# GpSimd in place of VectorE for the softmax weights of one attention

## The reference, cut to what matters

```python
def swa_sink_attention(q, k, v, sinks):          # heads 0 to 7
    ...
    p = jax.nn.softmax(jnp.concatenate([s, sink], axis=-1), axis=-1)[..., :-1]
    o = jnp.einsum('bnkgqs,bnskd->bnqkgd', p.astype(vb.dtype), vb)

def dsa_attention(q, k, v, iq, ik, iw):          # heads 8 to 15
    ...
    _, idx = lax.top_k(score, n_top)
    ...
    p = jax.nn.softmax(s, axis=-1)
    o = jnp.einsum('bhqk,bqkd->bqhd', p.astype(vg.dtype), vg)

def mixer_ab(h, cos, sin, w_in, q_norm, w_uq, w_uiq, sinks, w_out):
    ...
    return jnp.concatenate([ya, yb], axis=-1) @ w_out
```

## Time and profile before

| | |
|---|---|
| time, median of 3 runs | 1816.06 us (1815.35 to 1817.51) |
| profiled execution | 1816.24 us, of which the span of the engines 1814.3 us |
| PE busy | 1743.7 us, 96% of the span |
| DVE busy | 749.0 us, 41% |
| ACT busy | 526.5 us, 29% |
| POOL busy | 26.6 us, 1%, 36 instructions |
| mean granted TensorE clock | 0.992 |

### The profile page before, as it was taken

How to read it: one execution, slowest core, us unless ns; L and a number is a source line. 1 busy time by engine, 2 the same in 40 slices (tenths; PEclk the granted TensorE clock), 3 DMA queues, 4 the chain that set the end, 5 groups by cost and what they waited for, 6 DMA issues and landing times.

```text
span 1814.3 us, 24405 instructions
## 1 busy us (share of the span) xinstructions
PE 1743.7 (96%) x9906; PEld 1092.5 (60%) x9906; DVE 749.0 (41%) x1287; ACT 526.5 (29%) x698; POOL 26.6 (1%) x36
## 2 busy tenths in 40 slices
PE   8999999999999999999999999999899999999997
PEld 7688754444434434343434344375699888679986
DVE  4454342212212112121212121379865469676555
ACT  5344421111111111111111010248444453744442
POOL 0002000000000000000000000000000000000001
PEclk9999999999999999999999999998999999999999
DMA  9958899999999999999999999974355556435550
GB/s 350 348 212 336 316 404 426 428 427 428 428 428 428 428 428 428 429 429 428 428 429 428 429 429 429 418 282 177 116 186 185 192 194 228 153 116 185 185 208 24
DMA packets 96608, 587.43 MB, mean 324 GB/s; under 512 B 7150, under 2 KB 7364, under 8 KB 70948
## 3 DMA queue, kind: packets, MB, share of 16 engines
q1 hardware_dynamic: 95072, 582.27, 79.3%
q10 hardware_dynamic: 1476, 4.30, 0.7%
HBM read 585.51 MB, written 1.05 MB: 323 GB/s over the span
## 4 chain that ended last, share of the span: by engine, by line
PE 72%; DMA 20%; DVE 5%; ACT 2%; issue 1%; SPq 0%; DVEq 0%; ACTq 0%
PE bank L1274 31%; DMA ring<-in_w_gate_up 19%; PE bank L1587 15%; PE bank L1606 9%; PE bank L1533 4%; PE bank L1861 3%; PE bank L1353 1%; PE bank L1617 1%; PE bank L1265 1%; PE bank L1579 1%; DVE w_lo L565 1%; ACT arena L965 1%; DMA ring<-in_ada_w 1%; PE bank L1599 1%; PE bank L1988 0%
## 5 line engine op out<-in xcount | busy, mean ns | idle before, releaser
L1587 PE MATMUL bank<-ring,arena 128*64 128x512 f32 x2048 | 462.4, 597 | 28.4 <-DMA ring<-in_w_gate_up 27.8
L1587 PEld LDWEIGHTS bank<-ring,arena 128*64 128x64 f32 x2048 | 137.7, 136 | 319.3 <-issue 255.9
L1606 PE MATMUL bank<-ring,arena 128*64 128x512 f32 x1024 | 226.8, 595 | 3.3
L1274 PE MATMUL bank<-w_hi,arena_r 128*128 128x512 f32 x672 | 217.1, 391 | 1.9 <-DVE arena_r L2705 1.9
L565 DVE TENSOR_TENSOR w_lo<-ring,w_hi 128x4096 fp32r<-128x4096 f32 (+2 forms) x44 | 192.5, 4375 | 44.1 <-ACT w_hi L554 41.8
L2400 DVE TENSOR_SCALAR arena<-bank 128x512 f32<-128x512 f32 x32 | 22.1, 691 | 367.2 <-PE bank L1587 367.2
L963 ACT ACTIVATE arena<-arena,sb_tab 128x512 f32<-128x512 f32 x32 | 23.1, 722 | 508.7 <-DVE arena L2400 508.7
L554 ACT ACTIVATE w_hi<-ring 128x4096 fp32r<-128x4096 f32 (+2 forms) x43 | 152.3, 3583 | 31.6 <-DMA ring<-in_c_w_out 18.3
L1606 PEld LDWEIGHTS bank<-ring,arena 128*64 128x64 f32 x1024 | 71.9, 137 | 137.6 <-issue 132.1
L1274 PE MATMUL bank<-XT_r,w_hi 128*128 128x256 f32 x512 | 145.8, 285 | 4.4 <-DVE arena_r L2689 4.4
L1274 PE MATMUL bank<-arena_r,w_hi 128*128 128x256 f32 x512 | 144.9, 283 | 0.0
(11 more groups left out here) (415 smaller groups left out, 2104.6 us busy)
## 6 DMA issues: line engine op xcount, KB each, us to landing
ring<-in_w_gate_up SPq DMA_DIRECT2D x128, 2048.0 KB, 32.0
ring<-in_w_down SPq DMA_DIRECT2D x64, 2048.0 KB, 35.3
ring<-in_mlp_w SPq DMA_DIRECT2D x32, 2048.0 KB, 8.3
ring<-in_ada_w SPq DMA_DIRECT2D x21, 2048.0 KB, 13.1
ring<-in_c_w_in SPq DMA_DIRECT2D x6, 2048.0 KB, 7.7
ring<-in_w_in SPq DMA_DIRECT2D x4, 2048.0 KB, 8.8
ring<-in_w_v SPq DMA_DIRECT2D x2, 2048.0 KB, 9.6
ring<-in_w_out SPq DMA_DIRECT2D x2, 2048.0 KB, 11.9
```

What stands on the lines that cost most here:

```text
L1274: mm = pe.matmul(out, st[a], mv[b], start=start and a + b == 0, stop=stop and a == 1, skip_group_check=True)
L1587: mm = pe.matmul(B[m][CAP * h:CAP * h + CAP, :], xe[:, 2 * j + kl, :], w[:, kl, m * D + h * HW:m * D + (h + 1) * HW], start=False, stop=(j ...
L1606: mm = pe.matmul(B[2][CAP * h:CAP * h + CAP, :], hT[:, c, CAP * j:CAP * j + CAP], w[:, c, h * HW:(h + 1) * HW], start=(j == 0 and c == 0), ...
```

## The change

In attention `ab` alone, VectorE's weights step ends with the reciprocals, which raise a new semaphore `ab_recip`. GpSimd waits for it and multiplies in place, in four operations for each unit, one for each head and half of the queries' tokens: two of 128 x 128 and two of 128 x 256, each with one tensor input and one reciprocal per partition. The second and the fourth raise `p`. From unit 2 on VectorE waits before its reciprocals until GpSimd has done unit u-2, as their places are used in turn. GpSimd's loop over the 8 units stands between its operation L777 and its wait for `late_read` 2, so its four small operations on the last modulation come behind unit 7. The other attention, `cc`, stays as it is.

```diff
             last = mod[:, 3, :]
             pool.wait_ge(sem("late_read"), 1)
             pool.tensor_tensor(mod[:, 2, 16:24], mod[:, 2, 16:24], ada_bT[:, 64:72], ALU.add).then_inc(sem("late_mod"), 1)
+            for u in range(ATTNS["ab"][0]):
+                pool.wait_ge(sem("ab_recip"), u + 1)
+                c, sc = 4 * (u % 2), SCORES["ab"][u % 3]
+                for t, (a, b) in enumerate(((0, P), (P, 3 * P))):
+                    for h in range(2):
+                        i = 8 + c + 2 * t + h
+                        ins = pool.tensor_scalar(sc[:, h, a:b], sc[:, h, a:b], att[:, 0, i:i + 1], None, ALU.mult)
+                    ins.then_inc(sem("p"), 1)
             pool.wait_ge(sem("late_read"), 2)
...
                     dve.wait_ge(*upto(st, "e", exps_of(st, u + 1)))
                     if u < ATTNS[st][1]:
                         link(dve.tensor_tensor(att[:, 2, c:c + 4], att[:, 2, c:c + 4], att[:, 4, c:c + 4], ALU.add))
+                    if st == "ab":
+                        if u >= 2:
+                            dve.wait_ge(*upto(st, "p", 2 * u - 2))
+                        dve.reciprocal(att[:, 0, 8 + c:12 + c], att[:, 2, c:c + 4]).then_inc(sem("ab_recip"), 1)
+                        return
                     link(dve.reciprocal(att[:, 0, 8 + c:12 + c], att[:, 2, c:c + 4]))
```

## The result

The changed kernel takes 1822.65 us, median of 6 runs (1821.31 to 1823.72), against 1815.3 us for the kernel before (6 runs, 1812.4 to 1817.51): ratio 1.0042, interval 1.003 to 1.0054, some 7 us slower. Forecast were 1816.7 us and no difference that can be measured; the measured time lies above the range of 1815.2 to 1819.7 us. Timed twice more beside the kernel before, it was slower by a ratio of 1.0073 (1.0056 to 1.009) and 1.0056 (1.0039 to 1.0073), in the medians by 12.4 and 9.9 us.

What follows compares the result with a forecast made beforehand. No single engine was taken to bound the stage, but a chain of handovers up to VectorE's first split; 2d - 0.28 = +0.66 us on the median 1816.06 gave 1816.7 us, range 1815.2 to 1819.7.

Steps and rivals of the forecast that it cites:

- The price of GpSimd's four operations: Attention ab, each unit: 1.45 us priced from GpSimd's casts, bounds 0.8 and 2.5 us.
- Slow GpSimd without the collision: Rival: GpSimd takes 2.0 to 2.5 us per unit, +1.8 to +2.8 us, about 1819.0 us; chance 0.05.
- d: Added latency from reciprocal to finished weights, for each unit whose transposes wait: 1.53 us against 1.06, +0.47 us.
- 2d - 0.28: Whole attention: d at units 0 and 4, less unit 2's 0.28 us wait for VectorE; +0.66 us.
- with 0.4 us to spare: Unit 3: GpSimd done near 1262.4 us, before TensorE wants the weights at 1262.67 + 0.19; delay hidden.
- Unit 7: Its transposes move by 1.1 us, hidden in 2.86 us between TensorE's projection end and VectorE's last bank.
- Nothing: Unit 1: transposes stand behind a TensorE projection and are copied behind ScalarE's second 3.6 us rounding; no delay.
- The relief: Two multiplications off VectorE per unit, 8.2 us over 8 units, worth only 0.28 us at unit 2's transposes.
- rival gain: VectorE's relief reaches the end as ScalarE binds less; at most 3.1 us less, 1813.0 us; chance 0.05.
- The collision: Rival: from 2.5 us per unit, GpSimd's last operation of unit 7 stands behind VectorE's first split; +6.4 us, 1822.6; chance 0.13.
- The clock: Rival: longer waits at units 4 to 7 bring 7 us of TensorE at half speed, 3.3 us, 1820; chance 0.05.
- ScalarE stood idle between 1247 and 1266 us: Sign that the forecast is wrong: VectorE was then the bound, and the relief counts.

Runs made afterwards that it cites:

- e3_forms: Changed kernel with GpSimd's operations in four forms by unit: the change's, times a constant, plain copy, two-input multiplication by the broadcast reciprocal; 1818.29 us, one run.
- e8_tt: Changed kernel with two two-input multiplications by broadcast reciprocals per unit on GpSimd in place of four operations; 1816.14 us against 1814.01 of before, ratio 1.0012.
- e4_units13: Kernel before with GpSimd multiplying in units 1 and 3 only, VectorE in the others; 1814.88 us against 1813.84 of before, ratio 1.0003.
- e1_skip: Kernel before without the multiplications of attention ab on any engine, weights left unscaled; 1815.08 us against 1813.84 of before, ratio 1.0009.
- e10_split: Against the kernel before, each unit's small multiplication on GpSimd in two-input form, the large one on VectorE; 1815.1 us against 1813.98, ratio 1.0009.
- e9_beffill: Kernel before with TensorE turning the identity 12 times into bank 2 ahead of its wait for the last queries; 1815.61 us against 1814.01, ratio 1.0009.

## Why the prediction was wrong

- **The price of GpSimd's four operations** is the step that failed. What came is nearest to the rival "Slow GpSimd without the collision", which had a chance of 0.05, at a price above its 2.0 to 2.5 us. The forecast took 1.45 us, "as a cast is the nearest thing that it has shown", with a high end of 2.5; they take 2.98. The fixed part was about right (0.28 us an operation against 0.20), the slope was not: 2.5 ns an element against the casts' 0.84. A cast and a multiplication by a scalar look alike by their inputs, and by `e3_forms` the time does not go by inputs. I had taken the two-input subtraction's 2.25 ns as a bound from above, for no other reason than that two inputs should cost more than one. No row of the trace of before bounded this form from above, and the text should have said so and widened the range.
- **d.** The handover was right: the transposes of unit 0 came at 3.31 us, 1.29 + 2.0, and 2.98 + 0.08 - 1.06 = 2.0. In `e8_tt`, where d is 0.63, the formula 2d - 0.28 gives the section sum within 0.1 us.
- **The formula beyond its bounds.** At d = 2.0 it gives +3.7 us and the split came +5.0 us later at least. Unit 3 was hidden "with 0.4 us to spare", true only up to d = 0.9; in the second profile of the change it waited 1.07 us for GpSimd, and since ScalarE's copies of unit 3 stand ahead of its exponentials of unit 5, its delay and unit 5's d add up on that path (+5.2 us at the transposes of unit 5), past the path over unit 4 (+3.8). At a larger price the path changes, and the terms cannot just be scaled.
- **Unit 7** was put down as hidden in TensorE's 2.86 us to spare. The path that I left out runs over the last output copy and the remainder on VectorE, between the splits, which waited 0.81 us there: 0.9 us. At this price unit 1, "Nothing" in the forecast, costs 0.4 us too where unit 0 does not cover it (`e4_units13`).
- **The sum.** Priced at 2.98 us, the forecast's formula gives 3.7 us, the paths that it lacked some 1.3 more ahead of the split and 0.9 behind it: the 5.9 us that all three profiles have. The medians lost 7.3, 12.4 and 9.9 us; the part above 5.9 is not attributed run by run.
- **The relief.** "Worth 0.28 us, not 8.2": borne out. The second section shrank by 0.24 us where the clock was as before, and without any multiplication the third is as long as with all of them. The rival gain is refuted by `e1_skip`, as far as one profile and a median 1.2 us above before can do it.
- **The collision** with the first split, the rival at 1822.6 us, did not happen: no operation of unit 7 is stretched. Its point of decision was wrong. I had counted 2.57 us from the start of unit 7, but with GpSimd behind, both hang on the end of unit 6: the split comes 3.04 us after it, unit 7's work takes 2.96. In the first profile of the change the split begins 0.07 us behind GpSimd's last multiplication. What was caught is the small addition behind it (4.28 us), on which nothing in this stage waits. The Trainium skill, SBUF — State Buffer, "Who interferes with whom", says that a VectorE instruction with two SBUF inputs contends with a GpSimd instruction that reads SBUF. By that rule, the trace agrees: 4.28 us beside the split against 0.20, and 1.12 against 0.61 in `e10_split`. That 1822.6 us is the measured time is luck.
- **The clock** was a rival at 0.05, placed at units 4 to 7. It came, mostly elsewhere: between units 0 and 2, in 2 of 3 profiles, where the second section was 2.4 and 3.9 us longer than in the other one. Once it also fell behind the wait of unit 4 (1269.5 to 1273 us). In the kernel before, 7 and 10 us of low clock go with the same 13.96 us, which fits ScalarE's full queue hiding them; with 17 us the section was longer in every profile, and the forecast had no term for that. ScalarE stood idle between 1247 and 1266 us, which the forecast had given as a sign that VectorE was the bound; in the first profile it waited for TensorE (2.15 us before 1260.47 us), so the sign had a second reading.

The Trainium skill, GPSIMD Engine Reference, section 4.1, calls one-input operations roughly line-rate on this engine. The measurement agrees for the copy (0.83 ns an element) and decides otherwise for a multiplication by a scalar (2.5 ns an element, three times the copy's). The estimate that the prediction made from its section 3.1, 1.95 us a unit and +1.7 us in all, was nearer than mine and still short.

## What to carry to other kernels

An engine taken off a path is worth only what the next wait there allows, and a handover costs its whole latency at every place where a consumer stands ready: list these places before pricing the busy time. Price an operation on GpSimd by a row of the same operation, not of one with as many inputs; where none exists, no row bounds it from above until it is measured, and a form with two inputs may be the cheaper one. Where a sum holds because some unit has a few tenths to spare, say up to which price, for beyond it the path is another.

## What the runs showed of the hardware

- GpSimd, fp32, in place: a multiplication by a scalar costs 0.60 us for 128x128 and 0.92 us for 128x256 with a scalar per partition, 0.53 and 0.85 with a constant, a copy 0.29 and 0.40, a two-input multiplication with a broadcast second input 0.40 and 0.61 (all `e3_forms`), and 1.61 us for 128x256 and 128x512 together (`e8_tt`).
- A VectorE and a GpSimd multiplication, each with two SBUF inputs and begun 0.04 us apart, took 0.69 and 1.12 us (`e10_split`) against 0.69 and 0.61 alone; a GpSimd addition of 0.2 us beside a 4.42 us split took 4.28 (the changed kernel).
- TensorE's granted clock falls to 0.50 (the 1.2 GHz level) for 7 to 17 us around unit 0, with the same kernel at different times and lengths. In the changed kernel it stood at 0.50 from 1246 to 1253 us and for most of the next 7, with TensorE busy 7.00 of 7 us in both windows. Filling one idle gap of TensorE did not remove the fall (`e9_beffill`).
